# A two-block sequence model on one core: the linear attention's units put ahead of a step's delayed work, and a second buffer for its gates

## The reference

```python
proj = h @ w_in
(dn_q, dn_k, dn_v, dn_z, dn_a, dn_b, gl_q, gl_k, gl_v, gl_g, gl_r) = split(proj)
qkv = silu(causal_dwconv(concat([dn_q, dn_k, dn_v]), dn_conv))        # 4 taps, 12 chunks of 128 features
o_dn = gated_delta_rule(l2_norm(q), l2_norm(k), v, log_a, beta)       # chunks of 64 tokens
log_alpha = log_sigmoid(gl_r @ gla_w_gate2 + gla_b_gate) / GLA_TAU    # the "gates"
o_gla = gla_attention(gl_q, gl_k, gl_v, log_alpha)                    # chunks of 64 tokens
o_gla = rms_norm(o_gla, gla_norm_g) * silu(gl_g)
return concat([o_dn..., o_gla...]) @ w_o
```

## The kernel before

| step | linear attention | delayed work of the step |
|---|---|---|
| 7, 19 | prep(1), prep(2) | conv_silu of c 0, of c 1 |
| 11 | state1(0) | conv_silu of c 0 |
| 13, 21 | norm(0), state0(1) | length of c 0, of c 1 |
| 15 | scores(1) | unit_length of c 0, conv_silu of c 1 |
| 23 | state1(1) | unit_length of c 1, conv_silu of c 2 |
| 27 | scores(2) | conv_silu of c 2 |
| 29 | values(2) | length of c 2 |
| 32, 44, 56 | state0(2), state0(3), state0(4) | piece_out of c 3, c 5, c 6 |
| 36, 48 | norm(2), norm(3) | piece_out of c 4, c 5 |
| 40, 52 | values(3), values(4) | piece_out of c 4, c 6 |
| 60 | norm(4) | piece_out of c 7, ft_whole of half 0 |
| 61 | scores(5) | length of c 6 |
| 63 | values(5) | unit_length of c 6, conv_silu of c 7 |
| 67, 69 | state0(5), state1(5) | conv_silu of c 7, length of c 7 |
| 71 | norm(5) | unit_length of c 7, conv_silu of c 8 |
| 75, 79 | values(6), state0(6) | conv_silu of c 8, of c 9 |
| 83, 87, 91 | norm(6), values(7), state1(7) | conv_silu of c 9, c 10, c 10 |
| 92 | norm(7) | piece_out of c 11 |

## Time and profile before

### The profile page before, as it was taken

The page is one execution under the profiler, slowest core; times in us unless marked ns, Lnnn a source line. Parts: engine busy times, 40 slices in busy tenths (PEclk is TensorE's granted clock), DMA queues, the critical chain, the costliest instruction groups (busy, mean ns, idle before and its releaser), DMA issues.

```text
span 3052.8 us, 33545 instructions
## 1 busy us (share of the span) xinstructions
PE 2886.5 (95%) x13468; PEld 2240.8 (73%) x13468; DVE 1575.1 (52%) x2473; ACT 1018.4 (33%) x1583; POOL 787.2 (26%) x456
## 2 busy tenths in 40 slices
PE   6998899999989999999999999999989999999998
PEld 2776556666638888888886778788757888888886
DVE  7445544333586455456448565776445343333335
ACT  2446533223212222222223650565454222222112
POOL 3322111121224444444441213311010222222221
PEclk9999899999999999999999999999999999999999
DMA  7210012211341211111113212013211111111111
GB/s 261 80 35 21 21 35 69 69 56 61 139 145 42 76 49 49 49 49 49 49 49 97 63 55 85 15 31 124 84 35 36 56 50 50 48 49 50 49 51 55
DMA packets 199768, 193.61 MB, mean 63 GB/s; under 512 B 16167, under 2 KB 147647, under 8 KB 199615
## 3 DMA queue, kind: packets, MB, share of 16 engines
q1 hardware_dynamic: 197984, 187.09, 19.2%
q10 hardware_dynamic: 1631, 4.40, 0.4%
HBM read 175.43 MB, written 13.89 MB: 62 GB/s over the span
## 4 chain that ended last, share of the span: by engine, by line
PE 79%; DVE 10%; ACT 7%; issue 2%; DMA 1%; POOL 1%; SPq 0%; ACTq 0%; DVEq 0%; POOLq 0%
PE bank L1284 63%; PE bank L1629 2%; PE bank L1391 1%; PE bank L1432 1%; PE bank L1446 1%; PE bank L1613 1%; PE bank L1581 1%; PE bank L1397 1%; PE bank L1253 1%; DVE ffn_conv L2263 1%; PE bank L1277 1%; PE bank L1600 1%; DVE ffn_conv L2259 1%; PE bank L1648 0%; ACT square L2676 0%
## 5 line engine op out<-in xcount | busy, mean ns | idle before, releaser
L1284 PE MATMUL bank<-ft_hi,panel_lo 128*128 128x512 f32 x1312 | 467.5, 391 | 4.2 <-POOL panel_lo L3016 4.2
L3016 POOL TENSOR_TENSOR panel_lo<-panel,panelm_hi 128x1024 fp32r<-128x1024 f32 x64 | 153.3, 2397 | 583.3 <-ACT panelm_hi L2578 583.3
L1284 PEld LDWEIGHTS bank<-ft_hi,panel_lo 128*128 128x128 f32 x1312 | 247.3, 188 | 56.6 <-POOL panel_lo L3016 4.4
L1284 PE MATMUL bank<-ft_hi,panel_hi 128*128 128x512 f32 x704 | 274.2, 390 | 0.0
L1284 PE MATMUL bank<-ft_lo,panel_hi 128*128 128x512 f32 x704 | 274.1, 389 | 0.0
L2259 DVE TENSOR_SCALAR ffn_conv<-ffn_in,ffn_taps 128x512 f32<-128x512 f32 x88 | 113.8, 1293 | 280.3 <-ACT ffn_in L2851 280.2
L2529 DVE TENSOR_TENSOR resid<-resid,bank 128x512 f32<-128x512 f32 x256 | 174.8, 687 | 151.5 <-PE bank L1284 150.6
L3016 POOL TENSOR_TENSOR panel_lo<-panel,panel_hi 128x1024 fp32r<-128x1024 f32 x66 | 158.1, 2404 | 240.0 <-ACT panel_hi L2578 240.0
L1284 PE MATMUL bank<-ft,panel 128*128 128x512 f32 x416 | 197.4, 614 | 8.0 <-ACT mod_part L2711 4.7
L1284 PE MATMUL bank<-ftm_hi,panelm_hi 128*128 128x512 f32 x512 | 200.6, 392 | 2.4 <-DVE ftm_lo L1913 2.4
L1284 PE MATMUL bank<-ftm_lo,panelm_hi 128*128 128x512 f32 x512 | 200.4, 391 | 0.0
(11 more groups left out here) (499 smaller groups left out, 6114.6 us busy)
## 6 DMA issues: line engine op xcount, KB each, us to landing
panel<-in_w_in SPq DMA_DIRECT2D x52, 512.0 KB, 3.6
panel<-in_w_ada SPq DMA_DIRECT2D x48, 512.0 KB, 3.7
panel<-in_ffn_w_up SPq DMA_DIRECT2D x44, 512.0 KB, 3.6
panel<-in_w_mlp_in SPq DMA_DIRECT2D x32, 512.0 KB, 4.0
panel<-in_w_mlp_out SPq DMA_DIRECT2D x32, 512.0 KB, 3.5
panel<-in_w_o SPq DMA_DIRECT2D x24, 512.0 KB, 3.5
panel<-in_w_out SPq DMA_DIRECT2D x24, 512.0 KB, 3.5
panel<-in_ffn_w_down SPq DMA_DIRECT2D x22, 512.0 KB, 3.5
```

Source lines behind the costliest of these rows:

```text
L1284: m = te.matmul(ps, a, b, start=(start and j == 0), stop=(stop and j == len(pairs) - 1))
L3016: pool.tensor_tensor(lo, k.view(p), hi.bitcast(F32), ALU.subtract).then_inc(*g.new("halved_lo", p))
```

## The change

In `schedule`, a step's piece comes first, then the linear attention's units of that step, then the delayed work (`steps[1:]`). The list has the same units, and each queue the same work. `gla_gates` gets a `cum_tmp` for each half, the second at an address of its own; DVE evicts all four banks in half 0's unit, and half 1 no longer waits for `gla_sum` of half 0 to do so. ACT's stream has two table loads fewer.

```diff
     dense, done = spaced(dense), 0
     for m, steps in enumerate(dense):
-        for step in steps:
-            step()
+        if steps:
+            steps[0]()
         upto = len(gla_units) * (m + 1) // (len(dense) - 4)
         for _, n, s in gla_units[done:upto]:
             for what in GLA_BANKS.get(s, ()):
                 k.banks.take(("gla", n, what), (4,) if what == "o" else (5, 6, 7))
             k.unit("gla", n, s)
         done = max(done, upto)
+        for step in steps[1:]:
+            step()
...
-    k.cum_tmp = place("cum_tmp", [P, 2, BANK])
+    k.cum_tmp = [place("cum_tmp", [P, 2, BANK]), place("cum_tmp", [P, 2, BANK], at=start + 4 * D * 36 + 256)]
...
-        for c in range(2):
-            v.wait_ge(*v.filled("gate2", c, h))
-            if h:
-                v.wait_ge("gla_sum", h - 1)
-            evict(dve.tensor_scalar(k.cum_tmp[:, c, :], v.bank("gate2", c, h)[:], k.col("gla_b_gate", c), -1.0, ALU.add,
-                                    ALU.mult), "gate2", c, h)
+            for hh in range(HALVES):
+                for c in range(2):
+                    v.wait_ge(*v.filled("gate2", c, hh))
+                    evict(dve.tensor_scalar(k.cum_tmp[hh][:, c, :], v.bank("gate2", c, hh)[:], k.col("gla_b_gate", c), -1.0,
+                                            ALU.add, ALU.mult), "gate2", c, hh)
         v.wait_ge(*v.evicted("gate2", 0, h))
-        cum = k.cum[:, :, half(h)]
-        softplus("gla", k.cum_tmp[:], cum, v.evicted("gate2", 1, h), h)
+        cum, tmp = k.cum[:, :, half(h)], k.cum_tmp[h]
+        softplus("gla", tmp[:], cum, v.evicted("gate2", 1, h), h)
```

More of the change, by code:

```diff
@@ L2189, in gla_gates @@
         for c in range(2):
-            m = dve.tensor_tensor_scan(k.cum_tmp[:, c, :], k.keep[:], cum[:, c, :], 0.0, ALU.mult, ALU.add)
+            m = dve.tensor_tensor_scan(tmp[:, c, :], k.keep[:], cum[:, c, :], 0.0, ALU.mult, ALU.add)
         m.then_inc(*v.new("gla_scan", h))
         v.wait_ge("gla_scan", h)
-        dve.tensor_copy(cum, k.cum_tmp[:]).then_inc(*v.new("gla_sum", h))
+        dve.tensor_copy(cum, tmp[:]).then_inc(*v.new("gla_sum", h))
     def gla(n, s):
@@ L2811, in gla_gates @@
     def gla_gates(h):
-        softplus("gla", k.cum_tmp, h)
+        softplus("gla", k.cum_tmp[h], h)
     def gla(n, s):
```

## The result

| kernel | median, us | runs |
|---|---|---|
| before | 3052.18 (3048.41 to 3056.96) | 15 |
| changed | 3059.01 (3054.95 to 3062.99) | 15 |

The ratio is 1.0021, 95% interval 1.0014 to 1.0028: the change costs 6.4 us (4.3 to 8.5). The forecast was 3054.0 in a range of 3043 to 3061, so the time lies in the range, but the forecast cost of 2.9 us was too small. The outcome to which the forecast gave most, "the same within 0.2%" (0.60), was missed narrowly: the ratio lies just beyond that border. Its interval excludes that nothing changed. The forecast had said that less than 6.1 us could hardly be told from no change; these runs tell the difference to about 2 us. The profiled execution of the changed kernel took 3057.56 us with a span of 3056.3, so 3.5 more than that of before: less than the runs say.

A forecast was written before the change was run, and what follows sets the result against it. Bound by waits in TensorE's in-order stream, 115 to 430 us, and the lower clock behind them; shifts, gates' +2.1 included, net +2.9 at the delta stage: 3051.22 + 2.9 = 3054.0 us, range 3043 to 3061.

The forecast's parts named there:

- The gates: Gates' own buffer: 5.09 us wait goes, about 8 us wait for the values' low part ends at 149.6; +2.1 us.
- Step 15: scores(1) ahead of the lengths of c 0: transposes end at 205.95, values(1) starts at 208.7, ACT's copy +3.4 us.
- Step 19: prep(2) ahead of the silu of c 1: 7 us wait for POOL's squares until 225.3, +5.0 us.
- Step 32: state(2) ahead of c 3's convolution: TensorE goes on at 256.2 after 2 us wait; then scores(3) +1.4 in the middle.
- Steps 56 to 71: state(4) at 321.3; values(5) waits until 338.2; second squares' wait goes; values(6) at 373.9 behind 5 us.
- The end: Step 92, last copy, taps and silu: delta stage moves from 425.48 to 428.4, +2.9 us, carried to the program's end.
- the order's +0.8: Order of units, whole stretch: what the gates' +2.1 leaves of the forecast's total cost of 2.9 us.
- Rival 1: Faster: step 19's delay is smaller, state(2) starts near 249.5; 3047, or 3042 if values(5) and (6) wait little; chance 0.25.
- Rival 2: Slower: convolution-buffer copies behind norm become TensorE's wait at every tile, removing gains of 3.3 and 3.1; 3060.5 us; chance 0.18.
- Rival 3: Nothing: the new buffer and the new order cancel within a microsecond; 3051 us; chance 0.10.

The follow-up runs named there:

- norm behind: Changed kernel with norm alone put back behind a step's delayed work, other five units ahead, both gates' buffers; 3048.05 us, ratio 0.9997 to the kernel before.

## Why the prediction was right, and where its size was off

Step by step, by the marks of the first pair of profiles:

- **The gates.** Right in where it ends, wrong in the price. The wait for `cum_tmp` went and that for the low part came, ending at 149.51 (said: 149.6). It is 6.03 us long, not 8, since the gates began 0.56 us later and TensorE worked at a low clock from 120 to 124 us, and so arrived 2 us later. Of the +2.1, 1.6 showed at 179 us and none in the total of this part: -1.5 (-4.3 to +1.2).
- **Step 15.** Right: transposes at 205.96 (205.95), values(1) at 208.94 without a wait (208.7). The first agrees by luck: 0.56 us of the shift is the later start, for which the forecast had no term. Not in the text was a wait of 1.24 us for ACT's late copy, at 215.24.
- **Step 19.** Right: the squares' wait, 6.12 us until 226.12 (7 until 225.3). TensorE arrives at 220.0, not at 218.4. Here the rule of the Trainium skill (ScalarE: Activation LUTs, What ACT_TABLE_LOAD costs), a drain of 1.38 us behind a load, would have said 228.1. The changed kernel again shows the activation 1.29 us behind the start of the load (325.79 and 327.08), so no drain. That its total of 3057 is nearer to the 3059 measured is no support for it.
- **Step 32.** Right in the start, 257.02 (256.2), with 2.36 us of wait (2). Wrong in "does not run cold": 0.50 for 6 us behind it. In return norm(2), at 263.95, waits for nothing (2.7 said); in the second profile, with a shorter low stretch, it waits 1.27 us. The +1.4 in the middle became +1.8 at 290.35.
- **Steps 56 to 71.** Right: 321.47 (321.3), 338.73 behind 4.82 us (338.2 behind 5), no wait for the squares at 357, 374.48 behind 5.65 us (373.9 behind 5).
- **The end.** 429.03 (428.4), a wait of 4.79 us.

So the chain held to within 1.3 us at every mark of this profile; that, and not the place in a range which reaches over most of two rivals, is what speaks for the mechanism. **The step that was off is the last, the sum**: "3054.11 + 2.9", with all of it carried to the end, against 6.4 measured. Its two terms were off in opposite directions. The runs do not show the gates' +2.1; the order's +0.8 is 5.8 (2.7 to 8.5). The profiles say the same of the stretch up to the delta stage: the order alone lengthens it by 3.4 and 5.3 us against the two profiles of before, and the changed kernel, with the gates' buffer on top, is no longer than that (312.8 and 313.8, against 313.3).

Where the missing 3.5 us are can be said only roughly. By the two pairs of profiles the stretch is longer by 3.0 in one and by 5.8 in the other, 4.4 in the mean, which is 1.5 more than the forecast, and the rest of the program is longer by 0.8 (2627.3 twice, against 2627.3 and 2625.8). The forecast had started from a profile of before in which the clock had stayed low longer than in the other. The last 1.2 us are within the interval and stay open, and with two profiles of each kernel the other two figures are estimates.

**Rival 1** (faster, if the delay of step 19 stays small) named the gain rightly, though not for this kernel: the states alone give 9.2 us. **Rival 2** (3060.5) is nearer to the time than the forecast, but its mechanism is only half there. The waits for the masked scores behind norm's copies are long at tiles 5 and 6, where the forecast had them too, and 0.65 us or less at the others (0.65 at 404.44). The gains at 321 and 357, which it would have taken away, are there. **Rival 3** (nothing) is excluded by the interval.

What the forecast did not show is how large the terms are that cancel. Going from one kernel to the next, by the ratios and 3052 us:

| kernel | ratio to before | step, us |
|---|---|---|
| states ahead | 0.9970 | -9.2 |
| and scores, values | 0.9977 | +2.1 |
| and norm (with the gates' buffers) | 1.0006 | +8.9 |
| and prep: the change | 1.0021 | +4.6 |

Each step is uncertain by some 3 to 5 us, and the second is not told from nothing. The prices are not those of the units alone (norm alone +14.0, prep alone +3.1), nor independent of the way taken: prep put ahead before norm costs 6.1 (from 0.9977 to 0.9997), and then norm 7.3. Each wait changes what the next one finds.

## What to carry to other kernels

When one rule moves six kinds of work at once, price each kind by what it is put in front of in the in-order queues: here the state units, whose long waits were for their own update, gained 9 us, and two others cost more than that. Norm, a chain of activations with table loads between them, went ahead of a copy and of taps that TensorE's masked scores hang on; prep, four activations behind a table load, went ahead of a silu that TensorE's next sums hang on. Move only those that wait, and keep such chains behind the work that feeds other engines. A term of 2 us that rests on a low clock in one profile is no term yet: take a second profile of the same kernel before building on it.

## What the runs showed of the hardware

- How long the granted clock stays at the lower level behind a same wait is not fixed: to 366 us in one execution and about 363 in another behind 4.4 us (above). The long waits in the interleaved stretch themselves repeat to within 0.1 us (7.74 and 7.77, 6.07 and 6.07, 5.49 and 5.49, 4.39 and 4.40).
- Whether it falls at all is not fixed by the wait's length either. A wait of 2.36 us until 257.02 was followed by 6 us at 0.50 in the changed kernel. In its second profile (2.36 us until 257.72) and with norm behind (2.35 until 257.93) the clock is at 0.55 and 0.60, and at 0.62 and 0.53, in the windows 258 to 260 and 260 to 262, and full behind them. In the kernel with scores, values and states ahead, the same wait (2.35 us until 253.31) and even one of 3.38 us until 260.61 are followed by the full clock:

```profile
253.30:259.30 6.00, 3.92 (x20) 3.07 (x20) 5.10 (x5) 1.06 (x3) 2.90 (x2) 1.00 0.00 0
260.60:266.60 6.00, 5.99 (x24) 4.06 (x25) 3.45 (x5) 3.86 (x4) 0.17 (x1) 1.00 0.00 0
```

- So the forecast's rule of thumb, that a wait of 3 us or more costs 2 to 3 us more, is too simple in both directions: with the order alone 0.68 was granted for 5 us behind a wait of 1.46 us (above), and here the full clock behind 3.38 us. Nor is the cost always kept: with the gates' buffer alone, 0.8 of the 1.6 us lost by then was regained behind 212, where a later cold stretch was shorter.
- In the stretch before the gates' values, the windows of 2 us from 120 to 124 show a granted clock of 0.62 and 0.53 in the first profile of the changed kernel, and the second profile of the kernel before shows 0.78, 0.50 and 0.87 from 120 to 126. The first profile of the kernel before shows 1.00 from 118 to 126. With it goes the length of the wait for `cum_tmp`: 5.09 us at full clock, 3.51 in the second profile, and 1.9 where the clock is low from about 118 to 126 (norm alone ahead, prep alone ahead).
